# Rounded output-projection weights move into memory that attention frees, with changes at the seams of the expert stages

## The chip, the cores and the metric

The kernel runs on one core of a Trainium2 chip. The metric is the device time of one execution in microseconds; the median of three runs of the kernel before is 1046.08 us (1045.98 to 1046.68).

## The reference

256 tokens of width 1024 go through one block with block attention and a convolutional feed-forward part, and then through two layers of a second model. All is float32. Cut to what matters here:

```python
def second_block(x, mem, positions, ...):
    for i in range(2):
        proj = x @ (nsa_w_in if i == 0 else mla_w_in)
        mix = nsa_mixer(...) if i == 0 else mla_mixer(...)   # 12 heads of 64
        xa = memory_cross_attention(xq, mk, mv)              # 4 heads of 64
        y = jnp.concatenate([mix, xa], -1) @ w_out[i]        # output projection, 1024 x 1024
        x = layer_norm(DEEPNORM_ALPHA * x + y, ln_g[i, 0], ln_b[i, 0])
        f = hier_moe(x, w_grp, b_grp, w_exp, b_exp, w_gate, w_up, w_down)
        x = layer_norm(DEEPNORM_ALPHA * x + f, ln_g[i, 1], ln_b[i, 1])
    return x

def hier_moe(x, ...):          # 4 groups of 4 experts, each 1024 x 512, 1024 x 512, 512 x 1024
    # best group, best two experts in it, gates; then for all experts e
    hdn = silu(x @ w_gate[e]) * (x @ w_up[e]) * gate[:, e]
    return sum over e of hdn @ w_down[e]
```

## The kernel before

Five programs, one for each engine and one for the DMA queue of SyncE (SP), run side by side and meet only through semaphores. Each does its work strictly in the order in which it is written, and so does SP: a load that waits holds up all loads written behind it.

**Rounded weights.** The large projections are computed as three products of rounded parts. A loaded unit of weights (up to 2 MiB, in one of three slots w0 to w2, unit u in slot u % 3) is taken in pieces. For each, ScalarE makes the high part (`cast`, L2436, tile phi), VectorE the low part (`cut`, L1669, tile plo), and TensorE multiplies (`three`, L987). There are four places for such pieces, which lie in the memory of w3 and w4; piece p goes to place p % 4 and waits, through s_pc, until TensorE has done with piece p - 4. The output projection of the first layer is the units oa0 and oa1, that of the second ob0 and ob1, four pieces each.

**Loads of units.** `load(name)` (L751) waits until the unit three places before it in the list of names has been used up: for a unit in pieces this is s_cut at the number of its last piece, that is, VectorE has cut all its pieces (`consumed`, L743). The last names are n5, oa0, oa1, m0, m1, ob0, uq, ukv, ob1. SP's program runs (L881 to L884):

```python
expert_loads(0, ("n5", "oa0", "oa1"), ("m0", "m1", "ob0"))
for name in ("uq", "ukv", "ob1"):
    load(name)
expert_loads(1, ("uq", "ukv", "ob1"), ())
```

**Stages of a layer.** Input projections; attention(1) or attention(2), a pipeline over 16 units of two heads (scores on TensorE, row extremes on VectorE, exponentials on ScalarE, normalisation on GpSimd at L2844, transposes L1120, the product with the values, called PV, L1142); the output projection `out_proj` (L1054), whose first piece is already computed within the attention pipeline (`heads_proj`, L1122); a layer norm and the choice of experts; the expert stage; the last layer norm.

**The expert stage** (`few_tokens`, taken when no expert has more than 32 tokens of a tile) goes through 24 blocks in the order g0, u0, then g, d, u for each following pair of experts, and last d7. `gather` (L1381) picks the tokens of a pair, `project` computes g and u, `down` the second product, `scatter` (L1458) adds the result to the sum in psum[4] to psum[7]; `keep`, `keep_slots`, `keep_down` and `places` are the steps of ScalarE and VectorE between them, and s["rl"] and `residual` bring in the residual, in a rounded high and low part. A block reads four halves of 1 MiB, two for its first part and two for its second, so a stage reads 96 of them, n = 0 to 95.

**Places of halves.** 22 places (`halves`, L328) hold them: the slots, parts of arena and ring, spare, gain_rows, hT, yT and z. `FIRST[i]` says which place each of the first 22 halves takes. SP issues these in the order of the places (L833), each behind the wait for what the place held before: s_pv for the end of attention, s_pc for the end of the output projection. In the second layer the order is: place 0 and the four in slots 0 and 1; behind s_pv, the seven in arena, ring and gain_rows (places 5 to 11); behind the cuts of ob1 the two in slot 2 (12 and 13); behind the end of the output projection those in slots 3 and 4 (14 to 17), hT (18) and yT (19); then z (20) and ring (21). Half n of 22 and more takes the place of an earlier one and waits until TensorE has used that (`half_before`, s["wf"], which counts parts of blocks; s["wf"] = 2 is block g0 done).

## Time and profile before

| | us |
|---|---|
| median of three runs | 1046.08 |
| the profiled execution | 1041.19 |
| its span in the trace | 1039.4 |
| TensorE matmul busy | 995.2 (96%) |
| VectorE busy | 556.3 (54%) |
| ScalarE busy | 403.8 (39%) |
| GpSimd busy | 112.4 (11%) |
| read from HBM | 289.98 MB |

The span is the time between the first and the last instruction of the profiled execution; 1.8 us lie around it. Matmuls are pipelined and their ends are modelled, so a busy TensorE is not TensorE at its peak. A wait that ends for several semaphores is put down to the one that came last.

### The profile page before, as it was taken

Reading aid. Unit: us, or ns where it says so; the run is one execution under the profiler, and the core shown is the slowest. Engines: PE = TensorE matmul, PEld = TensorE weight load, DVE = VectorE, ACT = ScalarE, POOL = GpSimd, SP = SyncE. Lnnn points to the kernel's source line nnn. Section 1 sums busy time; section 2 is a strip of 40 time slices with the busy share of each in tenths; the row PEclk is TensorE's granted clock in tenths of the full one; section 3 lists DMA queues with packets and bytes.
Section 4 is the critical chain, followed back from the end, with each engine's and each line's share of the span. In section 5 each row is a group of like instructions: output and inputs, shape, how many; then the busy total and the mean of one; then the engine's idle time right before and its main releaser. Section 6 shows DMA issues by size and latency. Waiting matters only on the chain.

```text
span 1039.4 us, 15398 instructions
## 1 busy us (share of the span) xinstructions
PE 995.2 (96%) x5856; PEld 670.3 (64%) x5856; DVE 556.3 (54%) x1199; ACT 403.8 (39%) x791; POOL 112.4 (11%) x149
## 2 busy tenths in 40 slices
PE   7999999999999999899999999999999999999994
PEld 7978899999876888778634333337667733333331
DVE  5756656666447744765333333457665413434374
ACT  5565456656336455773212112123483312121220
POOL 0722101111001000250002000000131002000000
PEclk9999999999999999999999999999999999999998
DMA  9872676555355535409999999995348999999992
GB/s 328 206 244 86 208 231 222 179 195 211 122 202 195 161 116 202 184 8 362 420 421 410 422 421 420 423 404 207 135 181 317 372 423 410 420 422 421 422 411 107
DMA packets 94189, 292.29 MB, mean 281 GB/s; under 512 B 11214, under 2 KB 44158, under 8 KB 70558
## 3 DMA queue, kind: packets, MB, share of 16 engines
q1 hardware_dynamic: 93422, 289.54, 72.8%
q0 software_dynamic: 688, 1.71, 0.5%
q8 instruction: 49, 0.80, 0.3%
q14 instruction: 30, 0.25, 0.1%
HBM read 289.98 MB, written 1.25 MB: 280 GB/s over the span
## 4 chain that ended last, share of the span: by engine, by line
PE 81%; DVE 11%; issue 3%; DMA 2%; ACT 2%; POOL 0%; SPq 0%; DVEq 0%; POOLq 0%; ACTq 0%
PE ps L989 36%; PE ps L1425 16%; PE ps L1454 10%; DVE yTr L2263 4%; PE ps L1142 3%; PE ps L1097 2%; PE ps L1120 2%; PE ps L1397 2%; PE ps L931 2%; DMA w<-in_moe_w_down 1%; DVE plo L1674 1%; PE ps L1500 1%; PE ps L1270 1%; PE ps L938 1%; PE ps L1347 1%
## 5 line engine op out<-in xcount | busy, mean ns | idle before, releaser
L1674 DVE TENSOR_TENSOR plo<-w,phi 128x1024 fp32r<-128x1024 f32 (+3 forms) x147 | 177.0, 1224 | 127.7 <-ACT phi L2445 127.6
L2445 ACT CAST phi<-w 128x1024 fp32r<-128x1024 f32 (+3 forms) x147 | 148.6, 1034 | 132.8 <-PE ps L989 122.5
L1425 PE MATMUL ps<-w,arena 128*64 128x512 f32 x472 | 135.7, 595 | 0.2 <-DMA w<-in_moe_w_up 0.2
L989 PE MATMUL ps<-hTr,phi 128*128 128x256 f32 x472 | 131.1, 278 | 0.3 <-DVE yTr L1816 0.3
L989 PE MATMUL ps<-hTr,plo 128*128 128x256 f32 x472 | 130.5, 276 | 0.0
L989 PE MATMUL ps<-yTr,phi 128*128 128x256 f32 x472 | 130.5, 276 | 0.0
L2235 DVE CAST hots<-ps 128x256 fp32r<-128x256 f32 x16 | 6.8, 423 | 182.1 <-PE ps L1435 172.1
L989 PE MATMUL ps<-phi,hTr 128*128 128x512 f32 (+2 forms) x240 | 94.1, 392 | 0.8 <-issue 0.7
L989 PE MATMUL ps<-phi,yTr 128*128 128x512 f32 (+2 forms) x240 | 93.2, 388 | 0.0
L1425 PE MATMUL ps<-arena 128*64 128x512 f32 x280 | 89.3, 595 | 0.8 <-issue 0.7
L989 PEld LDWEIGHTS ps<-hTr,phi 128*128 128x128 f32 x472 | 88.6, 188 | 0.7 <-issue 0.4
L989 PEld LDWEIGHTS ps<-hTr,plo 128*128 128x128 f32 x472 | 88.7, 188 | 0.0
L989 PEld LDWEIGHTS ps<-yTr,phi 128*128 128x128 f32 x472 | 88.6, 188 | 0.0
L2263 DVE SCALAR_TENSOR_TENSOR yTr<-ps,small,yTr 32x512 fp32r<-32x512 f32 x112 | 83.7, 748 | 2.1
L1454 PE MATMUL ps<-w,ring 128*64 128x512 f32 x328 | 81.8, 593 | 0.8 <-ACT ring L2736 0.4
L1425 PEld LDWEIGHTS ps<-w,arena 128*64 128x64 f32 x472 | 41.3, 137 | 61.5 <-issue 60.2
L2713 ACT ACTIVATE yTr<-ps,small 128x512 fp32r<-128x512 f32 x60 | 36.7, 688 | 98.5 <-PE ps L1454 89.6
L2834 POOL TENSOR_TENSOR small<-small 128x1 f32<-128x1 f32 (+1 forms) x18 | 11.7, 650 | 460.7 <-DVE small L1716 355.8
L1454 PEld LDWEIGHTS ps<-w,ring 128*64 128x64 f32 x328 | 26.9, 137 | 45.7 <-issue 44.4
L989 PE MATMUL ps<-plo,hTr 128*128 128x512 f32 (+2 forms) x144 | 55.0, 382 | 0.0
L1425 PE MATMUL ps<-ring,arena 128*64 128x512 f32 x120 | 54.3, 595 | 0.0
L989 PEld LDWEIGHTS ps<-phi,hTr 128*128 128x128 f32 x240 | 45.1, 188 | 11.0 <-issue 2.7
(361 smaller groups left out, 1713.3 us busy)
## 6 DMA issues: line engine op xcount, KB each, us to landing
w<-in_moe_w_down SPq DMA_DIRECT2D x41, 1024.0 KB, 14.7
w<-in_moe_w_up SPq DMA_DIRECT2D x31, 1024.0 KB, 16.9
w<-in_moe_w_gate SPq DMA_DIRECT2D x28, 1024.0 KB, 15.1
w<-in_w_up SPq DMA_DIRECT2D x22, 1024.0 KB, 7.7
arena<-in_moe_w_gate SPq DMA_DIRECT2D x18, 1024.0 KB, 13.0
arena<-in_moe_w_up SPq DMA_DIRECT2D x17, 1024.0 KB, 11.5
arena<-in_moe_w_down SPq DMA_DIRECT2D x15, 1024.0 KB, 21.8
w<-in_w_out SPq DMA_DIRECT2D x6, 2048.0 KB, 9.7
```

The costliest lines, as they stand in the source:

```text
L931: e.matmul(bank[:, 0:width], ident, mask if width == 256 else ident, start=True, stop=True)
L989: ins_ = e.matmul(o, l[a], r[b], start=first and i == 0, stop=last and i == 2, skip_group_check=group)
L1097: ins_ = e.matmul(psum[2 * (u % 2) + j["half"]][:, q * 256:q * 256 + w], lq, kk, start=True, stop=True)
L1120: ins_ = e.transpose(bk[:, o * 128:o * 128 + 128], prob(j["J"])[:, c:c + 128], ident)
L1142: ins_ = e.matmul(ob[hp:hp + 64, t * 128:t * 128 + 128], *m[o], start=(o == 0), stop=(o == len(m) - 1))
L1397: ins_ = e.transpose(gathered(m, hf, b)[:, o:o + 128], x_block(t, 4 * hf + 2 * b + c), one_hots[:, t, :, t, :].bitcast(F32))
L1425: ins_ = e.matmul(bank[64 * ee:64 * ee + 64, :], xg[:, k, o:o + 64], half_view(i, kind, p, ee, ab)[:, c, :], start=(k == 0), stop=(k == 7))
L1454: ins_ = e.matmul(psum[2 + hf][64 * ee:64 * ee + 64, :], turned[:, o:o + 64], down_view(i, p, ee, f, hf), start=(f == 0), stop=(f == 3))
L1674: e.tensor_tensor(plo[:, 0:m], slots[u % 3][:, j * m:j * m + m], phi[:, 0:m].bitcast(F32), ALU.subtract).then_inc(s_cut)
L2263: ins_ = e.scalar_tensor_tensor(y_parts[t][other, part], psum[2 + hf][own_, :], slot_gate[own_, p:p + 1], y_parts[t][own_, part].bitcast(F ...
L2445: e.copy(pieces[p % 4][0][:, 0:m], slots[u % 3][:, j * m:j * m + m]).then_inc(s_cast)
L2713: ins_ = e.mul(y_parts[part][:, hf * 512:hf * 512 + 512], psum[2 + hf][:, :], slot_gate[:, p:p + 1])
```

## The change

- Four new places, 4 to 7, for rounded pieces: two in arena (6144 to 10240) and two in ring (1024 to 5120), declared as float32r tensors over the same memory. All eight pieces of oa and all eight of ob go there (`place_of`); all others keep places 0 to 3. `piece_at` gives the last piece before p in a place, for the waits.
- Pieces 0 and 1 of oa0 and ob0 are cast and cut within attention, at u = n to n + 2, the others behind it; the casts and cuts of these units that stood before the attention are gone (two of oa0, four of ob0). The first piece of the output projection is computed at u = n + 2 instead of n + 1.
- SP's first 22 expert loads go out in the order of `FREED`. Places 14 to 17 (slots 3 and 4) wait for the last pieces before oa0 or ob0; the arena and ring places which the new pieces cover, and 18 (hT), wait for pieces 4 to 7 of the projection. `FIRST` is adapted.
- `gather` waits for each half of psum by itself, and `scatter` and `gather` alternate in halves.
- VectorE forms the low part of the residual behind its product of block 7 instead of ahead of it, and TensorE adds it behind the first part of down(7).
- Halves 94 and 95 are loaded in two column halves each, the second ones counted by s_tail, and down(7), keep_down(7) and the last scatter work in three parts (`LAST`).

```diff
@@ -84,7 +84,12 @@
 MOVED = 7
-FIRST = ([0, 1, 2, 3, 4, 5, 6, 19, *range(7, 19), 20, 21], [0, 5, 6, 1, 2, 3, 4, 19, *range(7, 19), 20, 21])
+TWICE = 94
+FIRST = ([0, 1, 2, 3, 4, 14, 15, 19, 16, 17, 5, *range(9, 14), 6, 7, 8, 18, 20, 21],
+         [0, 5, 6, 1, 2, 3, 4, 19, *range(14, 18), 7, 11, 12, 13, 8, 9, 10, 18, 20, 21])
+FREED = ([*range(5), *range(14, 18), 5, *range(9, 14), 6, 7, 8, *range(18, 22)],
+         [0, *range(14, 18), *range(1, 8), 11, 12, 13, 8, 9, 10, *range(18, 22)])
+PLACES = ((6, 7, 8, 18), (8, 9, 10, 18))
@@ -487,6 +494,25 @@
+        pieces_of_ring = []
+        for a in (6144, 8192):
+            pieces.append([arena_r[:, b:b + 1024] for b in (a, a + 1024)])
+        for b in (1024, 2048, 3072, 4096):
+            pieces_of_ring.append(ring_r[:, b:b + 1024])
+        pieces += [pieces_of_ring[0:2], pieces_of_ring[2:4]]
+        heads = [first_piece(name) for name in ("oa0", "ob0")]
+
+        def place_of(p):
+
+            for p0 in heads:
+                if p0 <= p < p0 + 8:
+                    return 4 + (p - p0) % 4
+            return p % 4
+
+        def piece_at(at, p):
+
+            return max((q for q in range(p) if place_of(q) == at), default=None)
+
         def used(p, c):
@@ -591,6 +617,9 @@
             return s_wh[h], 16 * (loads_before(i, h) + own.index(n) + 1)
+
+        WHOLE = [(0, slice(0, 512), psum[2]), (1, slice(0, 512), psum[3])]
+        LAST = [WHOLE[0], (1, slice(0, 256), psum[3][:, 0:256]), (1, slice(256, 512), psum[1][:, 0:256])]
@@ -820,6 +849,14 @@
+            def last_halves(i, homes):
+
+                for piece in range(2):
+                    at = slice(256 * piece, 256 * piece + 256)
+                    for n, h in zip(range(TWICE, 96), homes):
+                        e.dma_start(halves[i][h].rearrange("p (c n) -> p c n", n=512)[:, :, at],
+                                    half_source(i, n)[:, :, at]).then_inc(s_tail if piece else s_wh[h], 16)
+
             def same_count(i, path):
@@ -830,7 +867,7 @@
                 s = s_m[i]
-                for n in range(NHALF):
+                for n in FREED[i]:
                     if i == 0 and n == 1:
@@ -843,14 +880,16 @@
                         e.wait_ge(*B.full("mt5", 1))
-                    if n == 5:
+                    if n == (5, 7)[i]:
                         e.wait_ge(s_pv, (40, 72)[i])
-                    elif n == 8:
+                    elif n == (9, 11)[i]:
                         e.wait_ge(s_pv, (48, 80)[i])
...
                         e.wait_ge(*consumed(held[2]))
-                    elif n == 14:
-                        e.wait_ge(s_pc, 2 * units[name_of[held[2]]]["pieces"][1])
+                    elif 14 <= n < 18:
+                        e.wait_ge(s_pc, 2 * piece_at(n - 14, heads[i]) + 2)
+                    elif n in PLACES[i]:
+                        e.wait_ge(s_pc, 2 * (heads[i] + 4 + PLACES[i].index(n)) + 2)
                     elif n == 20:
@@ -863,9 +902,11 @@
                 nc.switch_bb(f"few{i}_sp", before[i])
-                for n in range(NHALF, 96):
+                for n in range(NHALF, TWICE):
                     e.wait_ge(s["wf"], half_done(half_before(i, n)))
                     expert_half(i, n)
+                e.wait_ge(s["wf"], max(half_done(half_before(i, n)) for n in range(TWICE, 96)))
+                last_halves(i, [home(i, n) for n in range(TWICE, 96)])
                 if after:
@@ -1119,7 +1162,7 @@
                             ins_.then_inc(B.sem_full(f"t{a}", i))
-                    if u == (n + 1 if a else n + 2):
+                    if u == n + 2:
                         e.wait_ge(s_ex, tiles[jobs[-1]["J"] + 1])
@@ -1385,12 +1428,12 @@
                         e.wait_ge(s["pl"], m)
-                        e.wait_ge(s["y0"], 2 * (2 * m - 1))
-                        e.wait_ge(s["y1"], 2 * (2 * m - 1))
-                    else:
-                        e.wait_ge(s["xa"], 2 * m + 1)
-                        e.wait_ge(s["xb"], 2 * m + 1)
                     for b in range(2):
+                        if m and hf == 0:
+                            e.wait_ge(s["y0"], 2 * (2 * m - 1) - 1 + b)
+                            e.wait_ge(s["y1"], 2 * (2 * m - 1) - 1 + b)
+                        elif m:
+                            e.wait_ge(s["xb" if b else "xa"], 2 * m + 1)
                         for c in range(2):
@@ -1441,38 +1484,46 @@
                     e.wait_ge(s["xb"], 2 * min(4, (p + 1) // 2 + 1))
-                    for part in range(2):
+                    for part in range(2 if p < 7 else 3):
+                        if part == 1 and p == 7:
+                            e.wait_ge(s["rl"], 2)
+                            residual(1, 0)
+                            residual(1, 1)
                         for ee in range(2):
-                            e.wait_ge(*half_loaded(i, half_number("d", p, ee, part)))
+                            e.wait_ge(*half_loaded(i, half_number("d", p, ee, min(part, 1))))
+                        if part == 2:
+                            e.wait_ge(s_tail, 32 * (i + 1))
                         if p < 7:
-                            blocks = [(f, hf) for f in (2 * part, 2 * part + 1) for hf in range(2)]
+                            blocks = [(f, *WHOLE[hf]) for f in (2 * part, 2 * part + 1) for hf in range(2)]
                         else:
-                            blocks = [(f, part) for f in range(4)]
-                        for f, hf in blocks:
+                            blocks = [(f, *LAST[part]) for f in range(4)]
+                        for f, hf, at, bank in blocks:
                             for ee in range(2):
                                 o = f * 128 + ee * 64
-                                ins_ = e.matmul(psum[2 + hf][64 * ee:64 * ee + 64, :], turned[:, o:o + 64],
-                                                down_view(i, p, ee, f, hf), start=(f == 0), stop=(f == 3))
+                                ins_ = e.matmul(bank[64 * ee:64 * ee + 64, :], turned[:, o:o + 64],
+                                                down_view(i, p, ee, f, hf)[:, at], start=(f == 0), stop=(f == 3))
                         ins_.then_inc(s["wf"])
-                def scatter(p):
+                def scatter(p, halves_=(0, 1)):
                     e.wait_ge(s["bb"], p + 1)
-                    for hf in range(2):
-                        if p == 7 and hf:
-                            residual(1, 1)
+                    for hf in halves_:
                         e.wait_ge(s["y0"], 2 * p + hf + 1)
                         e.wait_ge(s["y1"], 2 * p + hf + 1)
-                        if p < 7:
-                            for t in range(2):
-                                ins_ = e.matmul(psum[4 + 2 * t + hf][:, :], hots[:, p % 2, t * 128:t * 128 + 128],
-                                                y_parts[t][:, hf * 512:hf * 512 + 512], start=(p == 0), stop=False)
-                            ins_.then_inc(s["sc"])
-                            continue
+                        for t in range(2):
+                            ins_ = e.matmul(psum[4 + 2 * t + hf][:, :], hots[:, p % 2, t * 128:t * 128 + 128],
+                                            y_parts[t][:, hf * 512:hf * 512 + 512], start=(p == 0), stop=False)
+                        ins_.then_inc(s["sc"])
+
+                def last_scatter():
+                    e.wait_ge(s["bb"], 8)
+                    for n, (hf, at, _) in enumerate(LAST):
+                        e.wait_ge(s["y0"], 15 + n)
+                        e.wait_ge(s["y1"], 15 + n)
                         for t in range(2):
                             for part in range(2):
-                                ins_ = e.matmul(psum[4 + 2 * t + hf][:, :], hots[:, p % 2, t * 128:t * 128 + 128],
-                                                y_parts[part][:, hf * 512:hf * 512 + 512], start=False,
-                                                stop=(part == 1))
+                                ins_ = e.matmul(psum[4 + 2 * t + hf][:, at], hots[:, 1, t * 128:t * 128 + 128],
+                                                y_parts[part][:, hf * 512:hf * 512 + 512][:, at], start=False,
+                                                stop=(part == 1 and n != 1))
                         ins_.then_inc(s["sc"])
@@ -1490,19 +1541,17 @@
                     if p in (1, 3, 5):
-                        gather(p // 2 + 1, 0)
-                    if p:
+                        for hf in range(2):
+                            scatter(p - 1, (hf,))
+                            gather(p // 2 + 1, hf)
+                    elif p:
                         scatter(p - 1)
-                    if p in (1, 3, 5):
-                        gather(p // 2 + 1, 1)
                     e.wait_ge(s["hm"], p + 1)
...
                     ins_.then_inc(s["tf"])
-                e.wait_ge(s["rl"], 2)
-                residual(1, 0)
                 down(7)
-                scatter(7)
+                last_scatter()
@@ -1792,6 +1843,9 @@
                         evac("pt", c, PcT2[c][0:NCMP, :, :], B.ap("pt", c)[0:NCMP, :].rearrange("p (h t) -> p h t", h=2))
+                    if a and u in (n + 1, n + 2):
+                        p = first_piece(("oa0", "ob0")[a - 1]) + u - n - 1
+                        cut(p, p + 1)
                     if a == 0 and u in (6, 7, 11, 12):
@@ -2025,7 +2079,6 @@
             ins_.then_inc(B.sem_empty("kt", 0))
-            cut(p0 + 5, p0 + 7)
             second_row(9, 3, 512, p0 + 3)
@@ -2289,14 +2342,14 @@
                         keep_down(p - 1)
+                    e.wait_ge(s["sl"], p + 1)
+                    e.wait_ge(s["wf"], block_done("u", p))
+                    e.tensor_tensor(middle, middle, psum[1][:, :], ALU.mult).then_inc(s["hm"])
                     if p == 7:
...
                                                    ALU.mult, ALU.subtract).then_inc(s["rl"])
-                    e.wait_ge(s["sl"], p + 1)
-                    e.wait_ge(s["wf"], block_done("u", p))
-                    e.tensor_tensor(middle, middle, psum[1][:, :], ALU.mult).then_inc(s["hm"])
                     if p == 0:
@@ -2355,8 +2408,6 @@
             evac("ck", 0, ckT[:, 0, :], B.ap("ck", 0)[:, 0:256], colv[:, KN:KN + 1])
-            p0 = first_piece("ob0")
-            cut(p0, p0 + 2)
@@ -2380,14 +2431,12 @@
                 project(n)
-                if n == 1:
-                    cut(p0 + 2, p0 + 4)
                 if n >= 2:
...
             attention(2, 0)
-            mixed("ob", 1, first_piece("ob0"), 4)
+            mixed("ob", 1, first_piece("ob0"), 2)
             experts(1)
@@ -2487,6 +2537,10 @@
                         evac("pt", c, PcT2[c][0:NCMP, :, :], B.ap("pt", c)[0:NCMP, :].rearrange("p (h t) -> p h t", h=2))
+                    if a and u in (n, n + 1):
+                        p = first_piece(("oa0", "ob0")[a - 1]) + u - n
+                        e.wait_ge(s_pv, (40, 72)[a - 1])
+                        cast(p, p + 1)
                     if a == 0 and u in (5, 6, 10, 11):
@@ -2774,8 +2829,6 @@
                  used(first_piece("m1") + 3, 1))
-            p0 = first_piece("ob0")
-            cast(p0, p0 + 2)
@@ -2799,15 +2852,13 @@
                 project(n)
-                if n == 1:
-                    cast(p0 + 2, p0 + 4)
                 if n >= 2:
...
             p0 = first_piece("ob0")
-            cast(p0 + 4, p0 + 8)
+            cast(p0 + 2, p0 + 8)
             experts(1)
```

## Rows read from the trace of the kernel before

**Rows 1.** The page: span, busy times of engines, DMA shares in 40 slices.
```profile
span 1039.4 us, 15398 instructions
...
PE 995.2 (96%) x5856; PEld 670.3 (64%) x5856; DVE 556.3 (54%) x1199; ACT 403.8 (39%) x791; POOL 112.4 (11%) x149
...
DMA  9872676555355535409999999995348999999992
```

**Rows 2.** Stretches: length, busy time by engine, clock, DMA share, GB/s.
```profile
810.90:1007.60 196.70, 191.09 (x936) 80.28 (x935) 78.84 (x173) 41.28 (x71) 6.79 (x7) 1.00 1.01 418
...
170.00:172.00 2.00, 2.00 (x20) 2.00 (x20) 1.74 (x3) 1.05 (x1) 0.00 (x0) 1.00 1.10 348
```

**Rows 3.** TensorE in order of time, end of second stage: start, us, ..., idle before.
```profile
1008.56 3.65 PE L1425 MATMUL ps<-w,arena 128*64 128x512 f32 x16 [0.19 <-DMA w<-in_moe_w_up]
...
1013.86 0.66 PE L1500 MATMUL ps<-cst,ring 128*128 128x128 f32 x4 [0.52 <-DVE ring L2299]
...
1015.19 3.65 PE L1454 MATMUL ps<-w,ring 128*64 128x512 f32 x16 [0.21 <-ACT ring L2736]
1019.25 3.65 PE L1454 MATMUL ps<-w,ring 128*64 128x512 f32 x16 [0.41 <-DMA w<-in_moe_w_down]
...
1024.57 1.18 PE L1473 MATMUL ps<-yTr,hots 128*128 128x512 f32 x4
```

**Rows 4.** SP's queue in order of time: start of issue, us, load.
```profile
745.28 0.37 SPq L756 DMA_DIRECT2D w<-in_w_out  x1
745.69 0.58 SPq L821 DMA_DIRECT2D spare<-in_moe_w_gate  x1
...
783.23 8.03 SPq L821 DMA_DIRECT2D arena<-in_moe_w_gate  x5
...
809.89 0.33 SPq L821 DMA_DIRECT2D w<-in_moe_w_down  x1
...
828.62 0.33 SPq L821 DMA_DIRECT2D spare<-in_moe_w_gate  x1
```

**Rows 5.** SP's waits, 740 to 800: us in total, times, longest.
```profile
SPq L756 <- DVE plo L1674: 16.3, 1, 16.3
```

**Rows 6.** The chain that ended last: TensorE's begin of the second expert stage.
```profile
824.99 5.29 PE ps L1425 x23
```

**Rows 7.** Ahead of attention 2: TensorE's waits (710 to 812), VectorE's cuts.
```profile
PE ps L1618 <- DVE arena L1658: 1.5, 2, 1.1
...
742.89 2.36 DVE L1674 TENSOR_TENSOR plo<-w,phi 128x1024 fp32r<-128x1024 f32 x2 [0.86 <-ACT phi L2445]
```

**Rows 8.** End of attention 2: TensorE, GpSimd, and the chain's projection.
```profile
784.52 0.63 PE L1120 MATMUL ps<-cst,gain_rows 128*128 128x128 f32 x4
...
785.10 1.04 POOL L2844 TENSOR_TENSOR gain_rows<-gain_rows,small 128x512 f32<-128x512 f32 x1 [0.72 <-DVE small L1786]
...
790.43 19.44 PE ps L989 x84
```

**Rows 9.** TensorE's waits in the first expert stage, 500 to 710.
```profile
PE ps L1397 <- DVE yTr L2263: 3.3, 3, 1.1
PE ps L1500 <- DVE ring L2299: 1.4, 2, 1.0
```

**Rows 10.** End of attention 1: TensorE, VectorE, ScalarE, SP in order of time.
```profile
472.60 0.50 PE L989 MATMUL ps<-phi,yTr 128*128 128x512 f32 x1
...
474.06 4.63 DVE L1674 TENSOR_TENSOR plo<-w,phi 128x1024 fp32r<-128x1024 f32 x4 [0.41 <-ACT phi L2445]
...
472.98 3.90 ACT L2445 CAST phi<-w 128x1024 fp32r<-128x1024 f32 x4
...
476.45 0.33 SPq L821 DMA_DIRECT2D w<-in_moe_w_gate  x1
```

**Rows 11.** DMA issues from 744 to 764: KB each, us from issue to landing.
```profile
w<-in_w_out SPq DMA_DIRECT2D x1, 2048.0 KB, 8.0
```

**Rows 12.** A stretch behind TensorE's last matmul, columns as in rows 2.
```profile
1030.00:1033.00 3.00, 0.00 (x0) 0.00 (x0) 2.84 (x7) 0.00 (x0) 0.55 (x1) 0.55 0.47 183
```

More of the change, by code:

```diff
@@ L234, in build @@
         with ExitStack() as same:
-            arena_r = same.enter_context(nc.sbuf_tensor("arena_r", [128, 4096], F32R))
+            arena_r = same.enter_context(nc.sbuf_tensor("arena_r", [128, 10240], F32R))
         arena = sb("arena", [128, ARENA])
+        with ExitStack() as same:
+            ring_r = same.enter_context(nc.sbuf_tensor("ring_r", [128, 5120], F32R))
         ring = sb("ring", [128, 5120])
@@ L904, in sync_program @@
                         e.wait_ge(s["uf"], 8 * p + 8)
-                    expert_half(i, n, h)
+                    if n < TWICE:
+                        expert_half(i, n, h)
+                last_halves(i, [many_loads[i][n - 96][1] for n in range(TWICE, 96)])
                 if after:
@@ L993, in cut @@
                 e.wait_ge(s_cut, p + 1)
-                return [a[:, 0:piece[p][2]] for a in pieces[p % 4]]
+                return [a[:, 0:piece[p][2]] for a in pieces[place_of(p)]]
             def tok3_steps(bks, pair, n, p0, steps, each=2, rows=None, ready=None):
@@ L1522, in down @@
                         e.wait_ge(*half_loaded(i, half_number("d", ex // 2, ex % 2, hf), True))
+                    if ex // 2 == 7:
+                        e.wait_ge(s_tail, 32 * (i + 1))
                     hd = yes[ex % 2]
@@ L1671, in cut @@
                     u, j, m = piece[p]
-                    phi, plo = pieces[p % 4]
+                    phi, plo = pieces[place_of(p)]
                     e.wait_ge(s_cast, p + 1)
@@ L2255, in keep_down @@
                     e.wait_ge(s["gv"], 2 * p + 2)
-                    for hf in range(2):
-                        part = slice(hf * 512, hf * 512 + 512)
-                        e.wait_ge(s["y0"], 2 * p + hf + 1)
+                    for n, (hf, at, bank) in enumerate(LAST if p == 7 else WHOLE):
+                        part = slice(hf * 512 + at.start, hf * 512 + at.stop)
+                        e.wait_ge(s["y0"], 2 * p + n + 1)
                         if p < 7:
@@ L2268, in keep_down @@
                             continue
-                        e.scalar_tensor_tensor(y_parts[1][:, part], psum[2 + hf][:, :], slot_gate[:, p:p + 1],
+                        e.scalar_tensor_tensor(y_parts[1][:, part], bank[:, :], slot_gate[:, p:p + 1],
                                                y_parts[0][:, part].bitcast(F32), ALU.mult,
@@ L2442, in cast @@
                         e.wait_ge(s_w[u % 3], 16 * units[u]["parts_so_far"])
-                    if p >= 4:
-                        e.wait_ge(s_pc, 2 * (p - 4) + 2)
-                    e.copy(pieces[p % 4][0][:, 0:m], slots[u % 3][:, j * m:j * m + m]).then_inc(s_cast)
+                    old = piece_at(place_of(p), p)
+                    if old is not None:
+                        e.wait_ge(s_pc, 2 * old + 2)
+                    e.copy(pieces[place_of(p)][0][:, 0:m], slots[u % 3][:, j * m:j * m + m]).then_inc(s_cast)
             def row_squares(t):
@@ L2656, in scalar_program @@
             p0 = first_piece("n3")
-            cast(p0 + 4, p0 + 7)
+            cast(p0 + 4, p0 + 5)
             first_row(8, 3, 512, p0 + 3)
@@ L2707, in keep_down @@
                     e.wait_ge(s["gv"], 2 * p + 2)
-                    for hf in range(2):
-                        e.wait_ge(s["wf"], block_done("d", p) - (p == 7 and hf == 0))
+                    for n, (hf, at, bank) in enumerate(LAST if p == 7 else WHOLE):
+                        e.wait_ge(s["wf"], 47 + n if p == 7 else block_done("d", p))
                         if p:
@@ L2712, in keep_down @@
                         for part in range(2 if p < 7 else 1):
-                            ins_ = e.mul(y_parts[part][:, hf * 512:hf * 512 + 512], psum[2 + hf][:, :], slot_gate[:, p:p + 1])
+                            ins_ = e.mul(y_parts[part][:, hf * 512 + at.start:hf * 512 + at.stop], bank[:, :],
+                                         slot_gate[:, p:p + 1])
                         ins_.then_inc(s["y0"])
```

6 lines of the change are left out of this document (3 added, 3 removed).

## The prediction, written before the result was known

> **What bounds the kernel now.** I read the page, then SP's queue and its waits, then the stretches round the two expert stages. TensorE is busy 96% of the 1039.4 us span [rows 1], so a gain must come out of TensorE's path; a loss needs only a transfer that comes late. The row of DMA shares shows full regions in both expert stages and nearly empty ones at the end of each attention [rows 1]. In the second expert stage DMA moves 418 GB/s for 196.7 us at a share of 1.01 [rows 2]: one half (1 MiB) every 1.048576 MB / 418 GB/s = 2.51 us. TensorE waits there 0.19 us for a w_up at 1008.56 and 0.41 us for the last w_down at 1019.25 [rows 3]: the halves land just in time. So the stage is bound twice, by TensorE and by the stream that carries 96 halves, and the stream ends at its start plus bytes over rate. Of every edit one must ask where it puts the start of that stream.
>
> The starts are in SP's queue [rows 4]. The first half of the second stage goes out at 745.69, directly behind the load of ob1 (745.28); others wait for attention (from 783.23), the rest for the end of the output projection (from 809.89). And ob1's load itself had waited 16.3 us, for a cut of VectorE (plo, L1674) [rows 5]: load() waits for consumed("ob0"), that is until all four pieces of ob0 are cut, since both units use one slot.
>
> **Part by part.** (1) The weights of oa and ob get four places in arena and ring, and the old four (slots 3 and 4) take expert halves before attention ends. That is good for the stream: at the end of the projection 18 of the 22 first halves are loaded or queued instead of 14. But the first place is free again only when block g0 is half done: SP issues that load at 828.62, 3.6 us after TensorE begins at 824.99 [rows 4, 6]. Now the 23rd half starts at 811.2 (809.89 and 1.3 us) + 8 x 2.51 = 831.3, 6.3 us behind TensorE's begin; afterwards at 3.6 + 1.3 = 4.9. More lead finds no place, so the stream gains 1.4 us, less 0.2 for the shorter rows of the last loads (348 GB/s in a stretch of w_up loads, whose rows are 1 KB [rows 2]; bounds of that 0 and 1): 1.2 us.
>
> (2) Pieces 0 and 1 of oa are no longer rounded before attention 1. VectorE waits for TensorE behind those two cuts anyway: 0 (bounds 1 us better, 0.5 worse). For ob four casts and cuts leave the stage ahead of attention 2; a pair of cuts of 2.36 us delays VectorE there, and TensorE's waits for L1658 are 1.5 us [rows 7]: 1.4 us gained (bounds 0.5 and 1.8).
>
> (3) They come back at the end of attention, where piece 0 of the projection moves behind the last transposes. It covered GpSimd's last normalisation, which ends at 785.10 + 1.04 = 786.14, while TensorE had its last transposes before it at 784.52 [rows 8]. Now TensorE does one unit's PV (0.6 us) and waits to 786.3, and piece 0 can start when its cut is done: the cast can begin at 784.45, 1.05 long, then VectorE's copy and the cut, 1.2, so about 786.9. With piece 0's 2.8 and 1.35 of PV, piece 1 starts at 791.1 instead of 790.43: +0.75 us, in each layer (bounds 0 and 2).
>
> (4) gather and scatter go in halves. Three gathers of a stage wait 1.1 us each for VectorE's L2263 [rows 9]; half 0 of both can fill that: 3.3 us a stage (bounds 0 and 4.2, with the shorter waits behind them). VectorE's product goes ahead of the residual's low part: of L1500's 1.4 us of waits in the first stage 1.0 is one wait, before down(7), and in the second 0.5 [rows 3, 9]. The column halves of the last loads leave 1.83 us of matmul behind the last landing instead of 3.65 [rows 3], and the scatter behind them 2.35 instead of 2.85, as the residual's matmuls move ahead. First stage: TensorE alone would gain 4.3 us, the stream allows 1.2 + 1.8 + 0.5 = 3.5. I take 3.2 (bounds 1 and 4.3).
>
> (5) **The wait that the change adds without a line in it.** ob0's pieces 2 and 3 are now cut only in mixed(), behind attention 2. ob1's load is unchanged and waits for them, and on SP's queue **all 22 first halves of the second stage stand behind it**. How late those cuts are, the first layer of this kernel shows, where oa's pieces 2 and 3 are cut behind attention already: casts from 472.98, cuts from 474.06 at 1.2 us each, and SP's load that needs them at 476.45, 3.85 us behind TensorE's 472.60 [rows 10]. So X = 791.1 + 3.85 = 794.95, less what was gained before it (3.2 + 1.4 - 0.75 = 3.85): **X = 791.1 instead of 745.28**.
>
> From X: ob1 lands 8.0 us after its issue [rows 11], the first half 2.4 us behind it. Two waits of TensorE follow. Piece 4 needs ob1: X + 8.0 + 2.3 for cast and cut = 801.4; TensorE would be ready at 791.1 - 3.85 + 3 x 2.78 (12 of the 84 matmuls in 19.44 us each [rows 8]) = 795.6: 5.8 us. Then n=7 (place 19, loaded 20th) lands at X + 10.4 + 19 x 2.51 = 849.2, while u0's second part asks for it at about 838: 11 us. Neither sets the end, the stream does: n=91, loaded 92nd, lands at X + 10.4 + 91 x 2.51 = 1029.9. TensorE could be there at 1018.8: 849.2, and from there the old path, 1008.56 less 835.6 (u0's second part at 824.99 + 10.6), less 3.3. Cover: 11 us. TensorE's last matmul ends at 1025.75 [rows 3], and between 1030 and 1033 its granted clock was 0.55 [rows 12], nearly all at 1.2 GHz of its two levels. Both waits are longer than that idle time; the few microseconds that the lower clock costs behind each go into the cover.
>
> **The sum.** Now n=91 is used from 1008.56 and the last scatter ends at 1025.75 [rows 3]: 17.2 us. Afterwards 6.1 to the start of down(7) (6.63 less 0.5), 3.65, 1.1 for residuals, 1.83 + 1.83, 2.35: 16.9 us. 1029.9 + 0.1 + 16.9 = 1046.9 against 1025.75: +21.15 us. What follows is unchanged. The profiled execution took 1041.19 us with its span of 1039.4; the median of the runs is 1046.08, 4.9 us above, and I add the difference to the median: **1067.2 us**.
>
> **Rivals.**
> A, **ob1's wait does not decide** (faster). Its point is 791.1 - 21.15 = 770: issued before that, the stream ends no later than now. If it is early enough for the stream to be no bound, 3.85 us before attention 2's end are gained, 3.2 in the second stage, less 0.75: 1046.1 - 6.3 = 1039.8. For it speaks that slot and queue idle in that time; against it that SP already waits 16.3 us for just these cuts [rows 5]. 4%.
> B, **TensorE becomes the bound**: the low clock lasts, or the two waits are longer than the cover. A block of 7 us at 1.2 GHz costs 7 more; the cover holds one and a half, six give 1067 + 31 = 1098. Against it: over the expert stage, with its short waits, the clock is 1.00 [rows 2]. 5%.
> C, **less is lost**: a rate 1% up (2.3 us less), cuts 1 us earlier, the first stage and the stage ahead of attention 2 at their upper bounds (1.5), 2 more from waits that I don't see: 1060 or a little below. 6%.
> D, **the stream is slower**: at the 348 GB/s of [rows 2] 91 halves take 46 us more, 1113. 1%: 196.7 us at 418 speak against it.
> The Trainium skill ("DMA: Bandwidth & Descriptors", Where 436 GB/s comes from) states that HBM binds such loads, at about 358 GB/s for a core; by it a half takes 2.93 us and the sum is 38 us longer, some 1105, an estimate from that page. The trace does not agree, with its 418 GB/s.
>
> **How the numbers follow.** The forecast (slower by 2%) has 84%. Its own bounds: gains before X between 1.5 and 6, tails between 0 and 2 in each layer, the rate 1% either way, together some 7 us. The range is 1060 to 1075; outside lie A, B, D and part of C. This kernel's measurement can tell 0.2% (2 us) from no change. Faster 0.04 (A), same 0.01 (the far end of C), slower 0.95.
>
> **What would show it.** The second layer's w<-in_w_out at about 791 on SP, after some 60 us of waiting for VectorE's plo; DMA all but empty from 730 to 791; TensorE waiting 6 us in the second output projection and 11 us in u0; DMA full to about 1040; the first expert stage 3 us shorter with L1397's waits gone. Wrong, if the second layer's first halves go out before attention 2 ends, or if the first stage is not shorter.

## The result

| | median | lowest to highest | profiled execution | its span | clock |
|---|---|---|---|---|---|
| before | 1046.03 us (4 runs) | 1041.35 to 1046.68 | 1041.19 us | 1039.4 us | 0.996 |
| after | 1070.24 us (4 runs) | 1065.09 to 1070.45 | 1070.20 us | 1068.4 us | 0.988 |

The change makes the kernel slower: ratio 1.0216, 95% interval 1.0195 to 1.0237, or 24.2 us of medians.

Both kernels run at one of **two levels** about 5 us apart (before 1041.3 or about 1046.3, after 1065.1 or 1070.3), and the profile of before fell on the lower one, that of after on the upper. The traces show where it is. The chains of waits, one row each (start, us, what):

```profile
129.73 119.70 PE ps L989 x1056
```
```profile
129.85 124.37 PE ps L1032 x1056
```

The same 1056 matmuls (128x256) take 119.70 us before and 124.37 us after, at a granted clock of 1.00 in both and with no wait of TensorE among them. At 249.26 and 254.06 us the next block starts. By 428 us the trace of after is 4.85 us late and has lost nothing else. So in what follows 4.85 us come off every time of the profile of after when it is set against one of before, and "level" means this. It is no effect of the change: before had runs near both levels in four of its five measurements.

From the page of after:

```profile
DMA  9864675564446428518899999992009999999993
```

The row of DMA shares shows the place: ahead of attention 2's end three digits are 2, 0, 0 where [rows 1] had 5, 3, 4; from there to the end it is full. SP's queue, in order of time (start of issue, us, load), and SP's waits (us in total, times, longest):

```profile
798.97 0.37 SPq L785 DMA_DIRECT2D w<-in_w_out  x1
799.38 0.58 SPq L850 DMA_DIRECT2D spare<-in_moe_w_gate  x1
```
```profile
SPq L785 <- DVE ring_r L1725: 65.3, 1, 65.3
```

ob1's load goes out at 798.97, having waited 65.3 us for VectorE's cut of ob0's last piece; in [rows 4] it went at 745.28 after 16.3 us [rows 5]. Behind it, 0.4 us later, comes the first of the 22 halves. The stretches (length, busy by engine, clock, DMA share, GB/s):

```profile
735.00:799.00 64.00, 60.18 (x381) 42.95 (x380) 40.13 (x165) 36.75 (x115) 17.17 (x24) 1.00 0.03 12
811.00:1040.40 229.40, 210.97 (x1005) 93.72 (x1005) 89.41 (x189) 41.94 (x71) 7.69 (x8) 0.97 1.01 419
```

For 64 us DMA moves 12 GB/s, then for 229 us 419 GB/s without a gap. The chain (start, us, what) and TensorE in order of time (its idle time ahead in brackets):

```profile
798.97 8.01 DMA w<-in_w_out
...
831.06 26.83 DMA yT<-in_moe_w_up
```
```profile
809.45 1.19 PE L1032 MATMUL ps<-arena_r,yTr 128*128 128x512 f32 x2 [5.73 <-DVE arena_r L1725]
...
858.03 1.08 PE L1468 MATMUL ps<-w,arena 128*64 128x512 f32 x1 [9.81 <-DMA yT<-in_moe_w_up]
...
1037.79 0.61 PE L1468 MATMUL ps<-arena 128*64 128x512 f32 x1 [0.27 <-DMA w<-in_moe_w_up]
...
1052.02 2.11 PE L1524 MATMUL ps<-yTr,hots 128*128 128x512 f32 x12
```

Both foreseen waits are there, 5.73 us for piece 4 and 9.81 us in u0. Half 91 is used at 1037.79, 238.8 us behind the load of ob1; TensorE's last matmul ends at 1054.13.

### The profile page after: what moved, and what is told of

Same layout as the page of the kernel before. It is cut to its first block, busy times and chain, and to the rows that moved or that the text cites. A ratio compares the mean times of both kernels' runs of the same rounds, so it can differ in the third digit from the quotient of the medians.

```text
span 1068.4 us, 15492 instructions
## 1 busy us (share of the span) xinstructions
PE 1007.3 (94%) x5896; PEld 682.7 (64%) x5896; DVE 556.6 (52%) x1201; ACT 403.9 (38%) x793; POOL 111.4 (10%) x149
## 4 chain that ended last, share of the span: by engine, by line
PE 78%; DMA 11%; DVE 6%; ACT 2%; issue 1%; SPq 1%; POOL 0%; POOLq 0%; DVEq 0%; ACTq 0%
PE ps L1032 35%; PE ps L1468 17%; PE ps L1503 8%; DMA w<-in_moe_w_up 5%; DMA yT<-in_moe_w_up 3%; DMA spare<-in_moe_w_up 3%; PE ps L1140 2%; PE ps L1185 2%; PE ps L1163 2%; PE ps L974 2%; PE ps L1440 1%; PE ps L1513 1%; SPq L850 1%; PE ps L1313 1%; DMA w<-in_w_out 1%
## 5 line engine op out<-in xcount | busy, mean ns | idle before, releaser
L1725 DVE TENSOR_TENSOR plo<-w,phi 128x1024 fp32r<-128x1024 f32 (+3 forms) x131 | 157.8, 1224 | 121.8 <-ACT phi L2495 121.7
L2495 ACT CAST phi<-w 128x1024 fp32r<-128x1024 f32 (+3 forms) x131 | 132.2, 1029 | 126.0 <-PE ps L1032 116.5
L1468 PE MATMUL ps<-w,arena 128*64 128x512 f32 x512 | 147.4, 599 | 12.6 <-DMA yT<-in_moe_w_up 9.8
L1468 PEld LDWEIGHTS ps<-w,arena 128*64 128x64 f32 x512 | 46.0, 138 | 82.4 <-issue 81.4
L1468 PE MATMUL ps<-arena 128*64 128x512 f32 x248 | 97.4, 596 | 1.2 <-DMA w<-in_moe_w_up 1.2
L1503 PE MATMUL ps<-w,ring 128*64 128x512 f32 x288 | 75.1, 594 | 4.5 <-DMA w<-in_moe_w_down 3.2
L2767 ACT ACTIVATE yTr<-ps,small 128x512 fp32r<-128x512 f32 (+1 forms) x62 | 37.1, 674 | 103.6 <-PE ps L1503 90.9
L1032 PE MATMUL ps<-phi,hTr 128*128 128x512 f32 (+2 forms) x176 | 68.6, 390 | 0.8 <-issue 0.7
L1032 PE MATMUL ps<-phi,yTr 128*128 128x512 f32 (+2 forms) x176 | 68.1, 387 | 0.0
L1503 PE MATMUL ps<-arena,ring 128*64 128x512 f32 (+1 forms) x168 | 54.1, 553 | 0.1
```

The costliest lines, as they stand in the source:

```text
L1032: ins_ = e.matmul(o, l[a], r[b], start=first and i == 0, stop=last and i == 2, skip_group_check=group)
L1468: ins_ = e.matmul(bank[64 * ee:64 * ee + 64, :], xg[:, k, o:o + 64], half_view(i, kind, p, ee, ab)[:, c, :], start=(k == 0), stop=(k == 7))
L1503: ins_ = e.matmul(bank[64 * ee:64 * ee + 64, :], turned[:, o:o + 64], down_view(i, p, ee, f, hf)[:, at], start=(f == 0), stop=(f == 3))
L1725: e.tensor_tensor(plo[:, 0:m], slots[u % 3][:, j * m:j * m + m], phi[:, 0:m].bitcast(F32), ALU.subtract).then_inc(s_cut)
L2495: e.copy(pieces[place_of(p)][0][:, 0:m], slots[u % 3][:, j * m:j * m + m]).then_inc(s_cast)
L2767: ins_ = e.mul(y_parts[part][:, hf * 512 + at.start:hf * 512 + at.stop], bank[:, :], slot_gate[:, p:p + 1])
```

## The experiments

Where nothing else is said a kernel's time is a median beside runs of before on the same chip, 1046.3 to 1047.0 us.

**ob as before, oa new.** The layer with the late cuts is put back:

```
-        heads = [first_piece(name) for name in ("oa0", "ob0")]
+        heads = [first_piece(name) for name in ("oa0",)]
 (second layer: FIRST, FREED, waits, casts and cuts of ob0 as in the kernel before)
```


> The changed kernel with the second layer's output projection (ob) and its expert places as before: ob0's four pieces are rounded ahead in the old places, ob1's load stands where it stood and finds them cut. oa's new places and all seam changes stay. Theory 1 (the loss is ob1's load that waits for ob0's late cuts, with 22 first halves behind it): the load goes out at about 745 to 750 us again and the loss is gone. From rows of the trace after: tail of attention 1 +1.5 us, first expert stage -1.7, last column halves -1.75 in the second stage: 1044 us (1041 to 1047). Theory 2 (the loss comes of the seam changes or of oa's places, the queue only moves a wait): 1060 or more.

1045.96 us (11 runs), ratio 0.9992 (0.9984 to 1.0001). ob1's load goes out at 750.34 and 24 us are gone, as theory 1 has it. Of the 2 us of gain that it hoped for, 1 at most is there.

**Seam changes alone**, with oa back as well:

```
-        heads = [first_piece(name) for name in ("oa0",)]
+        heads = []
 (first layer likewise)
```


> The changed kernel with oa and ob both as before (old places, pieces rounded ahead, piece 0 ahead of the last transposes): only the seam changes in the expert stages are left (gather and scatter in halves, VectorE's product ahead of the residual, last two loads and block in column halves). Theory 1: 1.75 us gained at the end of the second stage and 0.5 to 2 in the first, where without the early halves the stream is the bound: 1043 us (1041 to 1045). If a_oa_only is the faster of the two, oa's places pay; by the tail's 1.5 us against 1.2 of earlier halves they should not. Theory 2: near 1070 if the seams are to blame, 1046 if they do nothing.

1045.70 us (12 runs), ratio 0.9981 (0.9968 to 0.9993). The seam changes are no part of the loss. That they gain so little shows in TensorE's waits over the second expert stage of this kernel (us in total, times, longest):

```profile
PE ps L1505 <- DMA arena<-in_moe_w_down: 1.3, 1, 1.3
PE ps L1470 <- DMA ring<-in_moe_w_up: 0.9, 1, 0.9
...
PE ps L1505 <- DMA w<-in_moe_w_down: 0.6, 1, 0.6
```

The 3.3 us of waits for VectorE (those of [rows 9], the same in both expert stages of before) are no longer listed; 2.8 us of waits for DMA stand there instead. The edit works, and the stream takes the gain.

**ob1's load moved behind the early halves.** The changed kernel, one load moved in SP's queue:

```
-            for name in ("uq", "ukv", "ob1"):
+            for name in ("uq", "ukv"):
                 load(name)
...
                     elif n == 12:
+                        if i == 1:
+                            load("ob1")
                         e.wait_ge(*consumed(held[2]))
```


> The changed kernel with one line moved: SP issues ob1's load behind the early expert halves, directly ahead of the place that needs ob1 consumed. ob0's pieces 2 and 3 are still cut behind attention 2. Theory 1: the first halves go out from about 750 us, the stream is no longer the bound; what stays is TensorE's wait for ob1 (5.7 us in the trace after, with the lower clock behind it 7.9 us later into the second stage), less 3 us of gains in the stage: 1051 us (1048 to 1055). Theory 2 (the queue's order is harmless, the late cuts themselves cost the time): 1065 or more.

1052.47 us (4 runs), ratio 1.0057 (1.0043 to 1.0072). Eleven halves go out from 734.14 us on, two more at 787.13 and 795.63, and ob1's load at 799.38, as late as in the changed kernel. So **18 of the 24 us are the halves that queue behind that load**, and 6 the load itself: TensorE waits for its piece, and runs the next matmuls below full clock (the second row is a stretch, columns as above):

```profile
809.46 1.19 PE L1034 MATMUL ps<-arena_r,yTr 128*128 128x512 f32 x2 [5.33 <-DVE arena_r L1727]
```
```profile
805.00:810.00 5.00, 0.54 (x1) 0.50 (x2) 1.91 (x2) 2.99 (x4) 0.00 (x0) 0.62 0.27 98
```

**The kernel before, with ob1's load held.** One wait added, at three values:

```
-            for name in ("uq", "ukv", "ob1"):
+            for name in ("uq", "ukv"):
                 load(name)
+            e.wait_ge(s_pv, 80)        (then 54, then 66)
+            load("ob1")
```


> The kernel before with one wait added: SP issues ob1's load only when TensorE has done the last product of attention 2 (790.4 us in its trace). Nothing else is changed. Theory 1, by the prediction's own sum: half 91 lands at 790.5 + 10.4 + 91 x 2.51 = 1029.3 instead of being used at 1008.56, so +20.7 us: 1066.7 us (1063 to 1070). Theory 2 (DMA catches up, since TensorE is the bound): 1046 to 1050.

> The kernel before with ob1's load held until s_pv stands at 54: the product of attention 2 that TensorE starts at 767.62 us in its trace, 22.7 us later than the load goes out there. Theory 1 (a stream with a start and a rate): half 91 lands 239 us behind the issue, at 1007, and is used at 1008.56 now: nothing is lost, 1047 us (1046 to 1048.5), and the load's decisive point is about 769.5. Theory 2 (each us that the load is late costs one, from 745.28 on): 1068 or a good part of it.

> The same, held until s_pv stands at 66 (777.72 us in the trace of before, so X is 778.2). Theory 1: half 91 lands at 778.2 + 239 = 1017.2, 8.6 us behind its present use: 1055.5 us (1053 to 1057.5), and from there to the kernel that was held to the end of attention (1067.8, X 12.3 us later) one us for each. Theory 2 (a threshold: either the whole loss or none): 1047 or 1067.

| held until | load goes out | half 91's block starts | behind it | median | ratio |
|---|---|---|---|---|---|
| s_pv 54 | 769.99 (lower level) | 1010.34 | 240.4 | 1046.60 | 0.9995 (0.9981 to 1.0009) |
| s_pv 66 | 784.23 (upper) | 1024.21 | 240.0 | 1056.37 | 1.0085 (1.0061 to 1.0110) |
| s_pv 80 | 796.51 (upper) | 1035.61 | 239.1 | 1067.79 | 1.0198 (1.0183 to 1.0213) |
| changed kernel | 798.97 (upper) | 1037.79 | 238.8 | 1070.24 | 1.0216 (1.0195 to 1.0237) |

One row behind the table, TensorE of the kernel held to s_pv 80:

```profile
1035.61 3.65 PE L1427 MATMUL ps<-w,arena 128*64 128x512 f32 x16 [0.20 <-DMA w<-in_moe_w_up]
```

This is the whole loss in a kernel that has nothing of the change but the late load. A load 25 us late costs nothing; from about 770 us on, the point that the prediction named, each us costs nearly one (12.28 us later from the second row to the third, half 91 11.4 us later, the median 11.4 us up). No threshold shows, and DMA does not catch up. (In the first row 1.6 us of the 1010.34 come of a stretch of low clock in attention 1, shown further below; without them half 91 stands near 1008.56, where it stood.)

**Fewer bytes.** In the changed kernel six halves of the second layer are loaded by half. TensorE multiplies what stands in the places, so its work is the same and the kernel leaves out half of six weights:

```
+                if i == 1 and n in range(40, 46):
+                    m = src.shape[-1] // 2
+                    dst, src = (... [:, :, 0:m] or [:, 0:m] of both)
                 e.dma_start(dst, src).then_inc(s_wh[h], 16)
```


> The changed kernel with six of the second layer's 96 halves (40 to 45) loaded only by half their columns; TensorE multiplies what stands in the place, so its work is the same. Left out: half of these six weights. 3.1 MB less at 418 GB/s is 7.5 us of stream. Theory 1 (the stream sets the end, TensorE has 11 us of cover): 1070.2 - 7.5 = 1062.7 us. Rival (behind its two waits TensorE is the bound): 1068 to 1070.

1060.35 us is the middle of 1058.13, 1058.14, 1062.55 and 1062.95, two of each level. Level against level that is 7.0 us below 1065.09 and 7.5 below 1070.24: what the bytes are worth. The stream sets the end. TensorE has some 7 us of cover: its waits for halves from 1003 us on sum to 7.1 us in the changed kernel, and here one of 0.21 us is left.

**The wait filled.** c_ob1_behind with matmuls ahead of piece 4 that the next start=True overwrites:

```
+                keep_on(bks[0], 20)        (ob only; then 12)
                 for t in range(2):
                     for j in range(4):
                         pc = cut(p0 + 4 + j)
```


> c_ob1_behind with 20 matmuls into a bank that the next real matmul starts afresh, put where TensorE waits 5.3 us for ob1's fifth piece: TensorE is busy in the wait. Theory 1 (behind the wait TensorE works at its lower clock; 12 matmuls of 128x512 took 3.96 us instead of 2.8 and it is TensorE that sets the end of that kernel): 1.5 us come back, 1051 us against 1052.5. Rival (the stream sets the end there, so a faster restart changes nothing): 1052.5.

1051.80 us (4 runs: 1048.64, 1050.03, 1053.58, 1053.65): not settled by the times. TensorE in order of time, this kernel:

```profile
799.53 8.80 PE L976 MATMUL ps<-cst 128*128 128x256 f32 x40
807.98 0.82 PE L1034 MATMUL ps<-arena_r,yTr 128*128 128x512 f32 x2
```

The 20 took 8.80 us (they show as 40 records), 3.5 more than the wait. But from piece 4 to the gather of the expert stage there are now 23.56 us (807.98 to 831.54) instead of 25.09 (809.46 to 834.55): the lower clock behind that wait costs 1.5 us, as expected, and the fill had eaten it. Then 12:

> As g_kept_on with 12 matmuls in place of 20: there 20 took 8.80 us, 3.4 us more than the wait of 5.33 us that they fill, so their gain was eaten. 12 take 5.28 us. Theory 1 (TensorE's lower clock behind the wait costs 1.5 to 2 us, and TensorE sets the end of that kernel): 1050.5 to 1051 us, 1.5 to 2 below c_ob1_behind's 1052.5. Rival (the stream is the bound there too): 1052.5.

1047.45 us, ratio 1.0042 (1.0027 to 1.0056) beside a before of mostly lower level (1042.50), against c_ob1_behind's 1.0057 (1.0043 to 1.0072). The intervals overlap, and in its profile ob1's load took 10.3 us instead of 7.6, so TensorE waited 2.7 us all the same, its granted clock was 0.50 from 808.5 to 811.9, and piece 4 to the gather took 25.08 us as in c_ob1_behind. So this run did not fill the wait and tests nothing.

**Whole last loads.** b_seams_only, with each of the two last loads of a stage whole:

```
-                for piece in range(2):
-                    at = slice(256 * piece, 256 * piece + 256)
-                    for n, h in zip(range(TWICE, 96), homes):
-                        (load of columns `at`, counted on s_tail for the second piece)
+                for n, h in zip(range(TWICE, 96), homes):
+                    (load of all columns, counted on s_wh[h])
 (and no wait for s_tail)
```


> b_seams_only with the last two loads of each expert stage whole again, one semaphore each; the last block and the scatter stay in three parts. What it tells: the price of the column halves of the loads, which the prediction put at 1.8 us in the first stage. If that holds: 1045.7 + 2 x 1.8 = 1049.3 us. If the edit gains only what TensorE waited for the last landing (0.41 us in the kernel before, 0.6 in b_seams_only): at most 1 us for both stages, 1046 to 1046.7.

1046.51 us (12 runs), ratio 0.9995 (0.9981 to 1.0009), 0.8 us above b_seams_only, with intervals that overlap; the traces tell more. From the gather to the last scatter's end the second stage takes 203.92 us instead of 203.06, the first is as it was. In the second stage TensorE now waits 1.00 us for the last landing, in the first 0.17:

```profile
1020.68 3.67 PE L1500 MATMUL ps<-w,ring 128*64 128x256 f32 x32 [1.00 <-DMA w<-in_moe_w_down]
```

Column halves of the loads are worth 0.9 us in the second stage and next to nothing in the first, not 1.8 a stage.

**The pair of cuts apart.** b_seams_only, for casts (ScalarE) and cuts (VectorE) alike:

```
                 if n == 1:
-                    cut(p0 + 2, p0 + 4)
+                    cut(p0 + 2, p0 + 3)
                 if n >= 2:
                     turned_heads(n - 2)
+                if n == 3:
+                    cut(p0 + 3, p0 + 4)
```


> b_seams_only with the second pair of ob0's pieces (2 and 3) not rounded together behind project(1): piece 2 there, piece 3 behind turned_heads(1), where VectorE waits 1.97 us and ScalarE 2.45 us for TensorE in the trace of b_seams_only. Theory 1 (the pair of cuts of 2.36 us is what TensorE waits for, 1.2 us at its longest): 0.7 to 1.3 us gained on b_seams_only, 1044.7 us, and faster than the kernel before by 0.2%. Rival (another wait takes its place): as b_seams_only, 1045.7.

1044.22 us (12 runs), ratio 0.9979 (0.9965 to 0.9993). The median is 1.5 us below b_seams_only, but it was taken on another chip, where before is 0.6 us lower, and the ratios (0.9981 there) do not tell the two apart. The traces do, both at the upper level: from the turn behind the first expert stage to the gather of the second this kernel takes 109.12 us and b_seams_only 110.25, and TensorE's waits for L1711 fall from 1.6 to 1.0 us. The change itself had gained 1.3 us in this place by not rounding ob0 there: the same gain is to be had with the pieces rounded ahead.

**Each old place by itself.** On top of it:

```
-                    elif n == 14:
-                        e.wait_ge(s_pc, 2 * units[name_of[held[2]]]["pieces"][1])
+                    elif 14 <= n < 18:
+                        e.wait_ge(s_pc, 2 * (last piece of ob1 or oa1 in place n - 14) + 2)
 (FIRST and FREED: ... 13, 17, 14, 15, 16, 18 ...)
```


> f_cuts_apart with one more edit: the four old places of rounded weights are loaded with expert halves one by one, each when the last of its two pieces is used (the first some 4 us ahead of the projection's end), not all four behind the last; so the stream does not idle ahead of the stage (DMA share 0.78 from 800 to 812 us in the kernel before), and attention's end keeps its piece 0. In f_cuts_apart TensorE waits about 2.8 us for halves in each stage. Theory 1 (the stream is the bound, by its start): 1.2 us gained in each stage, as the 23rd half cannot start before the first place is free: 1041.8 us, 0.4% faster than before. Rival (the late halves are hidden, another landing is last): as f_cuts_apart, 1044.2.

1042.90 us (12 runs), **ratio 0.9960 (0.9946 to 0.9974): faster than both kernels**, and by 0.4% than the kernel before. Its interval overlaps that of f_cuts_apart. The stretch ahead of the second stage, of f_cuts_apart and of this kernel:

```profile
812.00:820.00 8.00, 8.00 (x61) 7.66 (x60) 4.31 (x14) 4.61 (x8) 0.91 (x1) 1.00 0.73 271
```
```profile
812.00:820.00 8.00, 8.00 (x61) 7.64 (x60) 3.96 (x13) 4.60 (x8) 0.91 (x1) 1.00 0.97 394
```

The gap in the stream is closed, and the second stage takes 0.9 us less (gather to the start of the last scatter, 200.06 against 200.94). The first stage did not gain (206.91 against 206.76 us from its gather to the first turn behind it), though its gap is closed too. TensorE's waits for halves there are the same 1.3 and 1.2 us in both kernels, so the halves it waits for did not come earlier; why stays open.

## Why the prediction was right, and where it was not

The forecast of 1067.2 us was 3.0 us low, inside its range. Level for level the span grew by 1068.4 - 4.85 - 1039.4 = 24.15 us against the 21.15 of the sum.

**What bounds the kernel** held: the stage is a stream with a start and a rate, and the question where an edit puts that start was the right one. The held loads and the fewer bytes show it, by nearly one us for one us. The cover was smaller than foreseen: 7.1 us of waits are left in the stage where the sum had 11 us, from which the lower clock behind the two waits was still to come off.

**(5), the wait without a line in the diff**, held in mechanism and in nearly each number. ob1's load goes out 3.86 us behind the start of piece 1 (3.85 foreseen, from the first layer's [rows 10]); ob1 lands in 8.0 us; TensorE waits 5.73 us (5.8) and 9.81 us (11); half 91 is used 238.8 us behind the issue (238.8), at 419 GB/s (418). From there to the last scatter's end there are 16.3 us, where the sum had 16.9. It was X that was wrong: 798.97 - 4.85 = 794.1 instead of 791.1, all of the 3.0 us. Behind the last matmul 0.6 us more pass than before, which the 0.6 us of the final chain cancel; I did not look into that.

**(4) is the term that failed**, by 1.5 us: the first stage was to become 3.2 us shorter, and from its gather to the first turn behind it only 1.7 went (207.36 to 205.67). Four kernels with the seam changes alone have 206.8 to 206.9 there, and before, held or not, 207.4 to 207.6: the seams give 0.65 us where "1.8 + 0.5" stood. The step that failed is "The column halves of the last loads leave 1.83 us of matmul behind the last landing instead of 3.65". It counts work behind a landing as if all of it had waited; TensorE waited 0.41 us for that landing in the second stage [rows 3] and not at all in the first. In the kernel with all seam changes but whole last loads it waits 1.00 us for that landing in the second stage and 0.17 us in the first, and against that kernel the split gained 0.86 us and nothing. The sum put the whole end of the second stage, this edit in it, at 0.3 us (17.2 to 16.9); the two parts disagree, and that should have been seen. Of the 3.0 us by which X was wrong 1.5 are this, 0.8 and 0.6 are (3) in the two layers, and 0.1 is (2).

**(1)** held: six kernels with oa's new places have a first stage of 205.6 to 205.9 us, 1.1 us below those without (1.2 foreseen).

**(2)** held: the stage ahead of attention 2 gained 1.3 us (1.4), oa's earlier pieces nothing.

**(3)** was too small in both layers. From the block behind the 1056 matmuls to the gather of the first stage there are 256.5 to 256.7 us in each of six kernels with the new places, 255.1 in before and about that in all but one of the others: 1.5 to 1.6 us instead of 0.75. (The kernel held to s_pv 54 has 256.7 too, for another reason: TensorE ran at its lower clock for 3.4 us there, which put it 1.6 us back, as the last section shows.) In the second layer it is 1.3 instead of the 0.67 us (791.1 less 790.43) that (3) rounds up to 0.75. VectorE, GpSimd and TensorE at the end of attention 2, changed kernel:

```profile
789.07 1.69 DVE L1725 TENSOR_TENSOR arena_r<-w,arena_r 128x1024 fp32r<-128x1024 f32 x1
...
791.35 1.21 DVE L1725 TENSOR_TENSOR arena_r<-w,arena_r 128x1024 fp32r<-128x1024 f32 x1
```
```profile
788.65 1.04 POOL L2895 TENSOR_TENSOR gain_rows<-gain_rows,small 128x512 f32<-128x512 f32 x1 [0.73 <-DVE small L1837]
```
```profile
791.16 0.70 PE L1032 MATMUL ps<-arena_r,yTr 128*128 128x512 f32 x2 [0.70 <-DVE arena_r L1725]
```

I priced the cut of piece 0 at 1.2 us. It takes 1.69, with GpSimd at work beside it until 789.69, and the next of the same size takes 1.21 without it; attention 1 shows the same pair (1.72 and 1.21). TensorE waits 0.70 us for the first. The Trainium skill ("GPSIMD Engine Reference", 1. Specifications) states that GpSimd shares its access to SBUF with VectorE and contends with VectorE's instructions of two SBUF inputs. The trace agrees, with 0.5 us in each layer; no run here moved that cut alone, so the cause is not isolated.

So the four places bring nothing in the first layer (1.1 us of stream against 1.5 us of tail) and cost 24 us in the second.

**Rivals.** A is out: its own decisive point, 770, was measured, and the load came 24 us behind it. B is out, by h_less_bytes: 7.5 us less stream, 7.0 to 7.5 us less time. C is out by the time itself, 1070.2 against 1060. D is out with 419 GB/s. There the prediction had set the 358 GB/s of the Trainium skill against the trace; another page of the Trainium skill ("Perfetto Trace Analysis", Roofline) says that this is a core's share when both of a pair pull, and that one alone can have more, up to some 435 GB/s. The trace agrees, with 419 over 229 us on one core.

## What to carry to other kernels

Follow each wait of an in-order queue to the last instruction that must have run, and then list what stands behind the waiting one: here four rounded pieces were put off by some 50 us to free four places of 1 MiB earlier, and the load of the next unit, with 22 MiB queued behind it, was put off with them. Where a stage is bound by a stream, only its start, its bytes and its rate count, and a gain on the computing engine comes back as a wait for the stream; so load each place when it is free, not four when the last is (0.9 us in one stage here, nothing in the other). Price an edit that splits a landing by what the engine waits for that landing (1.00 us waited, 0.86 gained), not by the work behind it.

## What the runs showed of the hardware that I had not expected

- The 1056 matmuls of 128x256 at full granted clock take 119.70 us in one execution and 124.37 us in another, or 276 and 281 ns for one by the groups of lines. Eight of the traced executions had the longer time (the next block starts at 254.06 to 255.11 us), six the shorter (249.26 to 249.97). No run told what chooses it.
- TensorE's granted clock can fall while it is busy. In the kernel held to s_pv 54 it was 1.00 from 410 to 417 us with TensorE busy 7.00 of 7.00 us, and then this stretch came:

```profile
417.70:421.10 3.40, 3.40 (x18) 3.40 (x18) 3.02 (x12) 0.71 (x2) 0.00 (x0) 0.50 1.02 422
```

  18 matmuls stand in it where before has 33 in the same stretch, at a clock of 1.00; TensorE is 1.57 us behind before at its end, and without a wait from 385 us on. No other traced execution has it, and no run told what starts it. Such a stretch in the one execution that is profiled looks like a cost of the edit.
- Loads that pile up hold SP itself: in the changed kernel ob1's load and nine halves went out in 6.7 us (798.97 to 805.67), and the thirteen halves behind them in 31.9 us, 2.45 us each instead of 0.4, near the 2.5 us in which one half is moved. It did no harm, since the stream stayed full.
- Round the one wait of 5.3 us in c_ob1_behind TensorE's granted clock was 0.62 from 805 to 810 us and 0.69 from 810 to 815; the way from there to the next gather took 1.5 us longer than with the wait filled.
